# Delta rule on one core: the second head of each pair inverted through the off-diagonal quadrants, P and T in two banks each without a second buffer

## The chip, the core and the metric

One core of a Trainium2 chip (trn2) runs the whole program in one launch. The metric is the device time of one execution in microseconds (us). The engines are PE (TensorE, with PEld for its weight loads), DVE (VectorE), ACT (ScalarE), POOL (GpSimd) and SP (SyncE, which issues DMAs). All arithmetic here is float32; the records of a float32 matmul come in two passes, each a load and a matmul.

## What is computed

The program is a stack of blocks; the part that matters is the RWKV-7 branch of each of the two layers of the second block: six heads of width 64, 1024 tokens, with a state that follows a delta rule.

```python
def step(state, inp):
    r_t, w_t, k_t, v_t, kk_t, a_t = inp
    sa = jnp.einsum('bhvk,bhk->bhv', state, -kk_t)
    state = (state * w_t[:, :, None, :]
             + sa[..., None] * (kk_t * a_t)[:, :, None, :]
             + v_t[..., None] * k_t[:, :, None, :])
    return state, jnp.einsum('bhvk,bhk->bhv', state, r_t)
```

The kernel works through it in chunks of 64 tokens. Within a chunk the recurrence is a triangular system of 64 equations per head, and its unit triangular matrix is inverted by doubling: the inverse T of diagonal blocks of 2 is known at once, and each of five levels (blocks of 4, 8, 16, 32, 64) makes from it a product P with the matrix, masked to the level's blocks, and from P the next T.

## The kernel before

The function `rwkv` (from L2259) is one block of instructions for all engines, written out by hand, with semaphores between them. A tile n is 128 tokens: two chunks of 64, one in SBUF partitions 0 to 63 and one in 64 to 127 (the two slices of `both`). There are NT = 8 tiles a layer, and the function runs once for each of two layers. The six heads are taken in NG = 3 pairs g; with LV = 5 levels that makes K = 15 steps, step k being level k // 3 of pair k % 3. PSUM is the one tensor `bk` of eight banks of 512 columns; the steps use banks 0 to 3, the preceding tile's outputs and state use banks 4 to 7.

A 64 x 64 matmul reads its operands from one half of the partitions and writes to a half. Before the change every matmul of the inversion reads and writes the same half (a diagonal quadrant of the 128 x 128 array). `chunks` (L2711 on) and `carry` also have matmuls that read one half and write the other (off-diagonal quadrants), into another bank than the diagonal ones.

PE's order for a tile n in the main loop at the end of the function: transposes of the inputs (`turns`, L2630), `low`, the preceding tile's `values`, scores of the pairs (`score`, L2642) with `solved` of the preceding tile between, `sums` of the next tile, then `turn_first` for each pair (L2651: the first T is the transpose of TT, its other form), and then the steps. `make_P` (L2661) forms P of both heads of the pair; `make_T` (L2672, L2674) forms the new T and TT; in the last level only TT (L2674). P alternates between banks 0 and 1 (`k % 2`), T between banks 2 and 3.

```python
make_P(n, 0)
for k in range(K):
    if k + 1 < K:
        make_P(n, k + 1)
    next(rest, None)
    make_T(n, k)
```

`rest` is the generator `tail(n - 1)`, the preceding tile's work in pieces: `outputs` (24 matmuls) before T(0), `chunks` of two heads (20 matmuls) before T(1), T(2) and T(3), `carry` (12 matmuls) before T(7) and T(10). The first tile of a layer has none of it.

DVE masks the scores (L2424), makes the first TT of each pair (`first_pairs`, L2429 and L2430), and then in each step masks P into PS (`take_P`, L2435). After take_P(k) it does one piece, and after every third step two, of `side(n)`, the next tile's element-wise work: `exponents` (L2398 to L2404), `keys` (L2381 to L2393, with `take_tr` L2441 among it) and from k = 8 on the four products of `scaled` (L2411 to L2417), which wait for `f_ready`. ACT copies the first T of each pair to SBUF (`take_first`, L2552) and in each step the new T and TT (`take_T`, L2558; L2560 in the last level). From k = 3 on it does pieces of its own `side(n)` after the copy: the next tile's exponentials (`exps`, L2509 and L2513, the last of which sets f_ready, after take_T(7)), `take_r2` (L2533), `take_S` (L2540), `take_y` (L2547). POOL forms five products per tile (`ends`, L2339 to L2343) once f_ready is there. The last tile of a layer has no next tile, so no side work.

What each step waits for, before: P(k) for the copy of that pair's T one level down (take_T(k - 3)); take_P(k) for P(k); T(k) for take_P(k) and, as its bank is reused, for take_T(k - 2); take_T(k) for T(k).

## Time and profile before

| | us |
|---|---|
| runs of the kernel before, median of 3 | 3772.6 (3770.73 to 3773.09) |
| the profiled execution | 3776.29 |
| its span, first to last instruction | 3775.0 |

The profile is that one execution. Times in rows are us from the span's start; a row of the timeline merges instructions of one line that follow each other, and gives its start, its length, the engine, the line, what it writes and reads, how many records, and in brackets how long its engine had been idle before and what ended that. Records of two operations that overlap are split into more rows, and a few matmul records can be missing. The first layer's stage of the delta rule runs from about 2058 to 2285, the second's from 3212 to 3435.

### The profile page before, as it was taken

The page shows a single profiled execution, that of the slowest core. Times are in us where ns is not written, and L with a number is a line of the kernel's source. Part 1 is how long each engine was busy: PE and PEld are TensorE (multiplying, and loading weights), DVE is VectorE, ACT ScalarE, POOL GpSimd, SP SyncE. Part 2 cuts the span into 40 slices and gives each one's busy share as a digit, 9 for nine tenths or more (in the row PEclk, how much of TensorE's full clock was granted, in tenths as well). Part 3 has the DMA queues.
Part 4 walks back from the last instruction along what each step waited for, and adds up shares of the span by engine and source line. Part 5 has one row for each costly group of instructions (what it writes and reads, how often), then busy time and mean ns, then how long its engine had stood idle before and what let it go on. Part 6 is the DMA issues. An engine that isn't in the chain of part 4 may idle for free. (4 is left out here: it accounts for less than half of the span.)

```text
span 3775.0 us, 57764 instructions
## 1 busy us (share of the span) xinstructions
PE 3532.6 (94%) x22960; PEld 2223.4 (59%) x22960; DVE 2164.6 (57%) x4615; ACT 1112.0 (29%) x2461; POOL 512.9 (14%) x326
## 2 busy tenths in 40 slices
PE   7999978999999997999998888998999998888998
PEld 5464444884488544655655776444655655777444
DVE  3255556446764573489976663342389976664343
ACT  2222344220122011320115555222230115555222
POOL 0020232000110010002221211210002221221210
PEclk9999989999999998999998999999999999999999
DMA  7343423234433442113341204211112331313310
GB/s 251 125 132 93 144 101 129 76 104 178 178 104 101 153 179 99 42 49 94 111 146 56 74 23 160 67 63 60 34 51 84 101 120 68 109 32 110 119 63 23
DMA packets 238731, 378.21 MB, mean 100 GB/s; under 512 B 30838, under 2 KB 168062, under 8 KB 237462
## 3 DMA queue, kind: packets, MB, share of 16 engines
q1 hardware_dynamic: 238478, 374.63, 30.2%
q8 instruction: 184, 3.01, 0.3%
q14 instruction: 69, 0.57, 0.1%
HBM read 291.89 MB, written 69.08 MB: 96 GB/s over the span
## 5 line engine op out<-in xcount | busy, mean ns | idle before, releaser
L3816 PE MATMUL win_acc<-across_room,across_hT 128*128 128x384 f32 (+3 forms) x3072 | 908.5, 456 | 3.8 <-PEq L83 3.8
L3816 PEld LDWEIGHTS win_acc<-across_room,across_hT 128*128 128x128 f32 x3072 | 561.4, 191 | 345.5 <-issue 15.5
L2828 DVE TENSOR_SCALAR_CACHE_REDUCE win_over<-d_sc,win_mid 128x384 uint8<-128x384 f32 (+5 forms) x384 | 337.9, 942 | 29.0 <-DVE win_mid L2839 28.6
L3877 ACT ACTIVATE layer_spare<-win_acc 128x384 f32<-128x384 f32 (+1 forms) x144 | 67.3, 467 | 575.4 <-PE win_acc L3816 575.4
L3652 PE MATMUL tail_wo<-tail_w_out,across_room 128*128 128x512 f32 x512 | 229.5, 603 | 6.6 <-DVE across_room L3484 6.6
L3663 PE MATMUL tail_wg<-tail_w_gate,across_room 128*128 128x512 f32 x512 | 224.5, 592 | 2.0 <-DVE across_room L3484 2.0
L3652 PEld LDWEIGHTS tail_wo<-tail_w_out,across_room 128*128 128x128 f32 x512 | 97.7, 193 | 126.0 <-issue 126.0
L1930 PE MATMUL mlp_bk<-across_hT,across_room 128*128 128x256 f32 x768 | 171.0, 379 | 0.0
L3663 PEld LDWEIGHTS tail_wg<-tail_w_gate,across_room 128*128 128x128 f32 x512 | 96.0, 190 | 117.2 <-issue 117.2
L1930 PEld LDWEIGHTS mlp_bk<-across_hT,across_room 128*128 128x128 f32 x768 | 145.9, 190 | 19.8
L3748 POOL TENSOR_TENSOR win_zp<-win_zp,layer_spare 128x3072 f32<-128x3072 f32 (+1 forms) x8 | 44.8, 5594 | 818.0 <-DMA win_zp<-s_z 818.0
L2674 PE MATMUL rwkv_bk<-rwkv_Tb,rwkv_PS 64*64 64x64 f32 x1920 | 127.5, 220 | 10.5 <-DVE rwkv_PS L2435 7.7
L2672 PE MATMUL rwkv_bk<-rwkv_PS,rwkv_Tb 64*64 64x64 f32 x1536 | 110.5, 224 | 24.4 <-DVE rwkv_PS L2435 20.7
L1930 PE MATMUL mlp_bk<-first_big,mlp_sums 128*128 128x256 f32 x512 | 118.8, 386 | 7.8 <-DVE across_room L1612 7.4
L1419 PE MATMUL mid_wo<-across_room,mid_yT 128*128 128x512 f32 x256 | 114.0, 600 | 3.5 <-ACT mid_yT L1360 3.5
L2435 DVE TENSOR_TENSOR rwkv_PS<-rwkv_bk,layer_early 128x128 f32<-128x128 f32 x240 | 67.8, 287 | 86.3 <-PE rwkv_bk L2661 84.7
L3960 DVE SCALAR_TENSOR_TENSOR d_sc<-win_rl,d_iw,d_sc 128x512 f32<-128x512 f32 (+3 forms) x140 | 92.1, 658 | 42.2 <-ACT win_rl L3893 29.1
L2558 ACT ACTIVATE rwkv_Tb<-rwkv_bk 128x256 f32<-128x256 f32 x192 | 73.6, 383 | 143.0 <-PE rwkv_bk L2674 141.9
L497 PE MATMUL zin_acc<-zin_wt,across_hT 128*128 128x272 f32 (+2 forms) x384 | 115.2, 457 | 0.0
L1930 PEld LDWEIGHTS mlp_bk<-first_big,mlp_sums 128*128 128x128 f32 x512 | 98.8, 194 | 22.5 <-issue 8.8
L1571 POOL TENSOR_TENSOR first_big<-first_big,mlp_rows 128x1024 f32<-128x1024 f32 x4 | 9.9, 2464 | 734.1 <-ACT first_big L1838 734.1
L2674 PEld LDWEIGHTS rwkv_bk<-rwkv_Tb,rwkv_PS 64*64 64x64 f32 x1920 | 100.9, 135 | 13.8 <-DVE rwkv_PS L2435 11.8
(578 smaller groups left out, 6630.4 us busy)
## 6 DMA issues: line engine op xcount, KB each, us to landing
across_room<-in_w SPq DMA_DIRECT2D x96, 1024.0 KB, 6.9
across_room<-in_w_in SPq DMA_DIRECT2D x18, 1536.0 KB, 8.2
s_z<-layer_spare SPq DMA_DIRECT2D x14, 1536.0 KB, 6.7
across_room<-in_w_ada SPq DMA_DIRECT2D x8, 2048.0 KB
across_hT<-s_z SPq DMA_DIRECT2D x16, 832.0 KB, 5.4
win_zp<-layer_spare SPq DMA_DIRECT2D x8, 1344.0 KB
tail_w_out<-in_w_out SPq DMA_DIRECT2D x4, 2048.0 KB, 10.8
tail_w_gate<-in_ple_w_gate SPq DMA_DIRECT2D x4, 2048.0 KB, 19.8
```

Source lines behind the costliest of these rows:

```text
L497: mm = pe.matmul(z, w, x, start=k == 0, stop=k == KC - 1)
L1419: mm = pe.matmul(wo[:, n % 2, c, :], yT[:, n % 2, q, :], w_out[:, c, q, :], start=q == 0, stop=q == KC - 1)
L1930: mm = pe.matmul(out, a[:, k, :], b[:, k, :], start=k == 0, stop=k == KC // 2 - 1)
L2435: dve.tensor_tensor(PS[:, 2 * g:2 * g + 2, :], blocks(bk[:, k % 2, 0:2 * HD]), bc_mid(levels[:, q, :], 2), ALU.mult).then_inc(p_out, 1)
L2558: act.activation(Tb[:, n % 2, g, :, :, :].rearrange("p a h t -> p (a h t)"), bk[:, 2 + k % 2, 0:4 * HD], ACT.Copy).then_inc(t_out, 1)
L2672: pe.matmul(bk[pr, 2 + k % 2, col(h)], TT_of(n, 2 * g + h, pr), PS[pr, 2 * g + h, :], start=True, stop=True)
L2674: mm = pe.matmul(bk[pr, 2 + k % 2, col(2 + h)], PS[pr, 2 * g + h, :], TT_of(n, 2 * g + h, pr), start=True, stop=True)
L2828: s.put(dve.tensor_scalar(over[q][:, :], sc[q][:, :], mid[:, q:q + 1], 0.0, ALU.is_gt, ALU.add, accum_out=cnt[:, q:q + 1]))
L3652: mm = pe.matmul(wo[:, c, :], yT[:, n % 2, q, :], W["out"][:, q, c * COL:(c + 1) * COL], start=q == 0, stop=q == KC - 1)
L3663: mm = pe.matmul(wg[:, c, :], xT[:, n % 2, q, :], W["gate"][:, q, c * COL:(c + 1) * COL], start=q == 0, stop=q == KC - 1)
L3816: mm = pe.matmul(acc[:, u % RING, 0:w], hT[:, k, t * P:(t + 1) * P], wt[:, i % 2, k, 0:w], start=k == 0, stop=k == KC - 1)
L3960: dve.scalar_tensor_tensor(x, y, iw, x, ALU.mult, ALU.add).then_inc(summed, 1)
```

## The change

Quoted are the edits that carry it; the two lambdas that swap which half of `Tb` holds T and which TT, and the index changes that follow from that, are left out where nothing else changes.

```diff
+        flat = bk[:, :, :].rearrange("p b c -> p (b c)")
+        T_AT, P_AT = 1 * 512, 3 * 512
+        swapped = [(slice(0, 64), slice(64, 128)), (slice(64, 128), slice(0, 64))]
...
-                    dve.tensor_tensor(mT[:, n % 2, h, :, :], blocks(bk[:, (3, 0, 1, 2, 3, 0)[h], 0:4 * HD]), masks[:, :, :], ALU.mult).then_inc(masked, 1)
+                    dve.tensor_tensor(mT[:, n % 2, h, :, :], blocks(bk[:, (0, 1, 2, 3, 0, 1)[h], 0:4 * HD]), masks[:, :, :], ALU.mult).then_inc(masked, 1)
...
-                    dve.tensor_tensor(PS[:, 2 * g:2 * g + 2, :], blocks(bk[:, k % 2, 0:2 * HD]), bc_mid(levels[:, q, :], 2),
+                    dve.tensor_tensor(PS[:, 2 * g:2 * g + 2, :], blocks(flat[:, P_AT - HD:P_AT + HD]), bc_mid(levels[:, q, :], 2),
...
-                    act.activation(xT[:, q, :, :], pairs(bk[:, q, :]), ACT.Copy).then_inc(xT_ready, 1)
+                    act.activation(xT[:, q, :, :], pairs(bk[:, 1 + q, :]), ACT.Copy).then_inc(xT_ready, 1)
...
-                def take_first(n, g):
-                    act.wait_ge(T_turned, START + NG * n + g + 1)
-                    act.activation(Tb[:, n % 2, g, 0, :, :], blocks(bk[:, 1 + g, 0:2 * HD]), ACT.Copy).then_inc(t_out, 1)
+                def take_first(n):
+                    act.wait_ge(T_turned, START + 2 * n + 1)
+                    act.activation(Tb[:, n % 2, 0, :, :, :].rearrange("p a h t -> p (a h t)")[:, HD:4 * HD], flat[:, P_AT - HD:P_AT + 2 * HD], ACT.Copy).then_inc(t_out, 1)
+
+                def take_others(n):
+                    act.wait_ge(T_turned, START + 2 * n + 2)
+                    act.activation(Tb[:, n % 2, 1:3, 0, 1, :], blocks(bk[:, 1, 0:2 * HD]), ACT.Copy)
+                    act.activation(Tb[:, n % 2, 1:3, 1, :, :].rearrange("p g h t -> p g (h t)"), pairs(bk[:, 0, 0:4 * HD]), ACT.Copy).then_inc(t_out, 2)
...
-                        act.activation(Tb[:, n % 2, g, :, :, :].rearrange("p a h t -> p (a h t)"), bk[:, 2 + k % 2, 0:4 * HD], ACT.Copy).then_inc(t_out, 1)
+                        act.activation(Tb[:, n % 2, g, :, :, :].rearrange("p a h t -> p (a h t)"), flat[:, T_AT - 3 * HD:T_AT + HD], ACT.Copy).then_inc(t_out, 1)
...
-                    banks = ((3, 0), (1, 2), (3, 0))[g]
+                    banks = ((0, 1), (2, 3), (0, 1))[g]
...
-                def turn_first(n, g):
-                    pe.wait_ge(TT_first, START + NG * n + g + 1)
-                    pe.wait_ge(masked, START + RWH * n + 3 + g)
+                def turn_first(n):
+                    pe.wait_ge(TT_first, START + NG * n + 1)
+                    pe.wait_ge(masked, START + RWH * n + 4)
+                    for pr, po in swapped:
+                        pe.matmul(flat[po, P_AT - HD:P_AT], id64[pr, :], TT_of(n, 1, pr), start=True, stop=True)
                     for h in range(2):
                         for pr in both:
-                            mm = pe.matmul(bk[pr, 1 + g, col(h)], Tb[pr, n % 2, g, 1, h, :], id64[pr, :], start=True, stop=True)
+                            mm = pe.matmul(flat[pr, P_AT + h * HD:P_AT + (h + 1) * HD], TT_of(n, h, pr), id64[pr, :], start=True, stop=True)
+                    mm.then_inc(T_turned, 1)
+
+                def turn_others(n):
+                    pe.wait_ge(TT_first, START + NG * n + NG)
+                    pe.wait_ge(masked, START + RWH * (n + 1))
+                    for g in (1, 2):
+                        for pr, po in swapped:
+                            pe.matmul(bk[po, 1, col(g - 1)], id64[pr, :], TT_of(n, 2 * g + 1, pr), start=True, stop=True)
+                        for h in range(2):
+                            for pr in both:
+                                mm = pe.matmul(bk[pr, 0, col(2 * g - 2 + h)], TT_of(n, 2 * g + h, pr), id64[pr, :], start=True, stop=True)
                     mm.then_inc(T_turned, 1)
 
                 def make_P(n, k):
                     g = k % NG
                     pe.wait_ge(t_out, START + (K + NG) * n + k + 1)
-                    if k == 0:
-                        pe.wait_ge(masked, START + RWH * (n + 1))
-                    for h in range(2):
-                        for pr in both:
-                            mm = pe.matmul(bk[pr, k % 2, col(h)], mT[pr, n % 2, 2 * g + h, 0, :], T_of(n, 2 * g + h, pr), start=True, stop=True)
+                    if k >= 1:
+                        pe.wait_ge(p_out, START + n * K + k)
+                    for pr, po in swapped:
+                        pe.matmul(flat[pr, P_AT - HD:P_AT], mT[pr, n % 2, 2 * g, 0, :], T_of(n, 2 * g, pr), start=True, stop=True)
+                        mm = pe.matmul(flat[po, P_AT:P_AT + HD], mT[pr, n % 2, 2 * g + 1, 0, :], T_of(n, 2 * g + 1, pr), start=True, stop=True)
                     mm.then_inc(p_made, 1)
 
                 def make_T(n, k):
                     g = k % NG
+                    a, b = 2 * g, 2 * g + 1
                     pe.wait_ge(p_out, START + n * K + k + 1)
-                    if k >= 2:
-                        pe.wait_ge(t_out, START + (K + NG) * n + NG + k - 1)
-                    for h in range(2):
-                        if k < K - NG:
+                    pe.wait_ge(t_out, START + (K + NG) * n + NG + k)
+                    if k < K - NG:
+                        for pr, po in swapped:
+                            pe.matmul(flat[pr, T_AT - HD:T_AT], TT_of(n, a, pr), PS[pr, a, :], start=True, stop=True)
+                            pe.matmul(flat[po, T_AT:T_AT + HD], TT_of(n, b, pr), PS[pr, b, :], start=True, stop=True)
+                        for h, at in ((a, 3), (b, 2)):
                             for pr in both:
-                                pe.matmul(bk[pr, 2 + k % 2, col(h)], TT_of(n, 2 * g + h, pr), PS[pr, 2 * g + h, :], start=True, stop=True)
-                        for pr in both:
-                            mm = pe.matmul(bk[pr, 2 + k % 2, col(2 + h)], PS[pr, 2 * g + h, :], TT_of(n, 2 * g + h, pr), start=True, stop=True)
+                                mm = pe.matmul(flat[pr, T_AT - at * HD:T_AT - at * HD + HD], PS[pr, h, :], TT_of(n, h, pr), start=True, stop=True)
+                    else:
+                        for pr, po in swapped:
+                            pe.matmul(flat[pr, T_AT - HD:T_AT], PS[pr, a, :], TT_of(n, a, pr), start=True, stop=True)
+                            mm = pe.matmul(flat[po, T_AT:T_AT + HD], PS[pr, b, :], TT_of(n, b, pr), start=True, stop=True)
                     mm.then_inc(t_made, 1)
...
-                        for g in range(NG):
-                            turn_first(n, g)
+                        turn_first(n)
+                        turn_others(n)
                         make_P(n, 0)
                         for k in range(K):
                             if k + 1 < K:
                                 make_P(n, k + 1)
+                            make_T(n, k)
                             next(rest, None)
-                            make_T(n, k)
                     for _ in rest:
                         pass
 
```

`flat` is `bk` with its banks as one row of columns, so that a product's two heads can lie at the end of one bank and the start of the next and be read as one operand: P at the border of banks 2 and 3, T and TT at that of banks 0 and 1. The first head's product goes to the lower bank from diagonal quadrants, the second head's to the upper bank from off-diagonal ones. Each of P and T has one place for all steps now, so make_P(k) waits for take_P(k - 1) and make_T(k) for take_T(k - 1). The second head's chunks lie with their halves swapped in one of its two forms, which is why turn_first and turn_others have two matmuls more for each pair. In PE's order, the piece of `rest` now comes after make_T(k).

## Rows read from the trace of the kernel before

**Rows 1.** Both stages by windows: busy us and records (PE, PEld, DVE, ACT, POOL), clock, DMA, GB/s.
```profile
2058.00:2285.00 227.00, 198.26 (x5441) 175.34 (x5443) 135.73 (x342) 117.41 (x275) 53.88 (x48) 0.99 0.21 61
3212.00:3435.00 223.00, 198.80 (x5467) 175.61 (x5468) 135.79 (x342) 117.12 (x275) 54.41 (x49) 0.99 0.22 62
```

**Rows 2.** Timeline of ACT, tile n = 2 of the second layer (first take_P at 3274.46).
```profile
3276.56 0.38 ACT L2558 ACTIVATE rwkv_Tb<-rwkv_bk 128x256 f32<-128x256 f32 x1 [2.31 <-PE rwkv_bk L2674]
...
3280.76 0.38 ACT L2558 ACTIVATE rwkv_Tb<-rwkv_bk 128x256 f32<-128x256 f32 x1 [1.02 <-PE rwkv_bk L2674]
...
3285.12 0.83 ACT L2513 ACTIVATE layer_spare<-layer_spare 128x768 f32<-128x768 f32 x1
...
3292.24 0.28 ACT L2560 ACTIVATE rwkv_Tb<-rwkv_bk 128x128 f32<-128x128 f32 x1 [0.24 <-PE rwkv_bk L2674]
```

**Rows 3.** Timeline of DVE, the same tile.
```profile
3274.46 0.29 DVE L2435 TENSOR_TENSOR rwkv_PS<-rwkv_bk,layer_early 128x128 f32<-128x128 f32 x1 [1.19 <-PE rwkv_bk L2661]
...
3285.99 0.56 DVE L2411 TENSOR_TENSOR layer_spare<-across_hT,layer_spare 128x384 f32<-128x384 f32 x1 [1.34 <-ACT layer_spare L2513]
3286.46 0.28 DVE L2435 TENSOR_TENSOR rwkv_PS<-rwkv_bk,layer_early 128x128 f32<-128x128 f32 x1
3286.66 1.17 DVE L2413 TENSOR_TENSOR layer_spare<-across_hT,layer_spare 128x384 f32<-128x384 f32 x1
...
3289.05 0.28 DVE L2435 TENSOR_TENSOR rwkv_PS<-rwkv_bk,layer_early 128x128 f32<-128x128 f32 x1
...
3290.34 0.47 DVE L2435 TENSOR_TENSOR rwkv_PS<-rwkv_bk,layer_early 128x128 f32<-128x128 f32 x2
```

**Rows 4.** Timeline of PE, the same tile, steps 1 and 2.
```profile
3275.88 0.28 PE L2672 MATMUL rwkv_bk<-rwkv_PS,rwkv_Tb 64*64 64x64 f32 x4
...
3276.34 0.34 PE L2661 MATMUL rwkv_bk<-rwkv_Tb,rwkv_mT 64*64 64x64 f32 x5
3276.47 0.27 PE L2717 MATMUL rwkv_bk<-rwkv_uw,rwkv_be 64*64 64x64 f32 x1
...
3276.82 0.27 PE L2717 MATMUL rwkv_bk<-rwkv_uw,rwkv_be 64*64 64x64 f32 x1
...
3277.28 0.28 PE L2672 MATMUL rwkv_bk<-rwkv_PS,rwkv_Tb 64*64 64x64 f32 x4
```

**Rows 5.** Timeline of PE, the same tile, the first P and a late step.
```profile
3273.96 0.68 PE L2661 MATMUL rwkv_bk<-rwkv_Tb,rwkv_mT 64*64 64x64 f32 x16 [0.19 <-ACT rwkv_Tb L2552]
...
3289.38 0.33 PE L2672 MATMUL rwkv_bk<-rwkv_PS,rwkv_Tb 64*64 64x64 f32 x4 [0.16 <-DVE rwkv_PS L2435]
```

**Rows 6.** Timeline of DVE, first tile of the second layer.
```profile
3223.12 0.29 DVE L2435 TENSOR_TENSOR rwkv_PS<-rwkv_bk,layer_early 128x128 f32<-128x128 f32 x1 [1.01 <-PE rwkv_bk L2661]
...
3223.91 0.29 DVE L2435 TENSOR_TENSOR rwkv_PS<-rwkv_bk,layer_early 128x128 f32<-128x128 f32 x1
```

**Rows 7.** Timeline of ACT, first tile of the second layer, the last exponential.
```profile
3230.44 0.84 ACT L2513 ACTIVATE layer_spare<-layer_spare 128x768 f32<-128x768 f32 x1
```

**Rows 8.** Timeline of DVE, last tile of the first layer.
```profile
2270.29 0.29 DVE L2435 TENSOR_TENSOR rwkv_PS<-rwkv_bk,layer_early 128x128 f32<-128x128 f32 x1
2270.99 0.29 DVE L2435 TENSOR_TENSOR rwkv_PS<-rwkv_bk,layer_early 128x128 f32<-128x128 f32 x1 [0.41 <-PE rwkv_bk L2661]
```

**Rows 9.** Windows: busy us and records by engine, clock, DMA share, GB/s.
```profile
2160.10:2163.50 3.40, 1.80 (x59) 1.66 (x55) 1.35 (x4) 1.21 (x3) 0.00 (x0) 1.00 0.19 69
2163.50:2166.90 3.40, 2.99 (x59) 2.81 (x57) 2.22 (x5) 2.23 (x5) 2.09 (x2) 0.50 0.02 5
3285.00:3290.40 5.40, 3.95 (x121) 3.64 (x115) 4.42 (x8) 2.77 (x8) 4.28 (x4) 1.00 0.01 3
```

**Rows 10.** Timeline of PE around the fall of the clock, first layer.
```profile
2163.22 0.21 PE L2674 MATMUL rwkv_bk<-rwkv_Tb,rwkv_PS 64*64 64x64 f32 x1 [1.60 <-issue]
...
2163.71 0.52 PE L2674 MATMUL rwkv_bk<-rwkv_Tb,rwkv_PS 64*64 64x64 f32 x4
2163.93 0.52 PE L2672 MATMUL rwkv_bk<-rwkv_PS,rwkv_Tb 64*64 64x64 f32 x4
```

More of the change, by code:

```diff
@@ L2299, in rwkv @@
         both = (slice(0, 64), slice(64, 128))
-        T_of = lambda n, h, pr: Tb[pr, n % 2, h // 2, 0, h % 2, :]
-        TT_of = lambda n, h, pr: Tb[pr, n % 2, h // 2, 1, h % 2, :]
+        T_of = lambda n, h, pr: Tb[pr, n % 2, h // 2, 1, h % 2, :]
+        TT_of = lambda n, h, pr: Tb[pr, n % 2, h // 2, 0, h % 2, :]
+        flat = bk[:, :, :].rearrange("p b c -> p (b c)")
+        T_AT, P_AT = 1 * 512, 3 * 512
+        swapped = [(slice(0, 64), slice(64, 128)), (slice(64, 128), slice(0, 64))]
         with ph.block() as block:
@@ L2429, in first_pairs @@
                     s(dve.scalar_tensor_tensor(L, L, -1.0, bc_mid(id64[:, :], 2), ALU.mult, ALU.add))
-                    dve.tensor_tensor(Tb[:, n % 2, g, 1, :, :], L, bc_mid(first[:, :], 2), ALU.mult).then_inc(TT_first, 1)
+                    dve.tensor_tensor(Tb[:, n % 2, g, 0, :, :], L, bc_mid(first[:, :], 2), ALU.mult).then_inc(TT_first, 1)
                 def take_P(n, k):
@@ L2557, in take_T @@
                     if k < K - NG:
-                        act.activation(Tb[:, n % 2, g, :, :, :].rearrange("p a h t -> p (a h t)"), bk[:, 2 + k % 2, 0:4 * HD], ACT.Copy).then_inc(t_out, 1)
+                        act.activation(Tb[:, n % 2, g, :, :, :].rearrange("p a h t -> p (a h t)"), flat[:, T_AT - 3 * HD:T_AT + HD], ACT.Copy).then_inc(t_out, 1)
                     else:
-                        act.activation(Tb[:, n % 2, g, 1, :, :], blocks(bk[:, 2 + k % 2, 2 * HD:4 * HD]), ACT.Copy).then_inc(t_out, 1)
+                        act.activation(Tb[:, n % 2, g, 0, :, :], blocks(flat[:, T_AT - HD:T_AT + HD]), ACT.Copy).then_inc(t_out, 1)
                 def side(n):
@@ L2591, in _ @@
                         if n < NT:
-                            for g in range(NG):
-                                take_first(n, g)
+                            take_first(n)
+                            take_others(n)
                             for k in range(K):
@@ L2629, in turns @@
                         for m in range(4):
-                            mm = pe.transpose(bk[:, q, m * P:(m + 1) * P], x4[:, m, q * P:(q + 1) * P], ident[:, :])
+                            mm = pe.transpose(bk[:, 1 + q, m * P:(m + 1) * P], x4[:, m, q * P:(q + 1) * P], ident[:, :])
                         mm.then_inc(turned, 1)
                 def score(n, g):
-                    banks = ((3, 0), (1, 2), (3, 0))[g]
+                    banks = ((0, 1), (2, 3), (0, 1))[g]
                     if g < 2:
@@ L2776, in _ @@
                     if n < NT:
-                        for g in range(NG):
-                            turn_first(n, g)
+                        turn_first(n)
+                        turn_others(n)
                         make_P(n, 0)
```

## The prediction

> **What bounds the kernel now.** I read the page's busy line first, then the windows of the two stages that the change touches, then one tile of the second layer, engine by engine. The delta rule fills 450 us of the 3775 us span (two layers, eight tiles of 128 tokens each); PE is busy 397 of them, at a clock of 0.99 [rows 1]. So a share of PE's time looks worth saving, but one tile shows that PE bounds only part of the stage. A tile takes 450/16 = 28 us: a head of transposes, scores and masks, and then, for 18 us, 15 steps k (five levels for each of three pairs of heads). A step is a product P, its masking by DVE (take_P), a product T and its copy by ACT (take_T).
>
> The steps have three limits. *Early (k = 0 to 4)* PE sets the pace, because the preceding tile's outputs and chunks are done between the steps: the first copy of T starts at 3276.56 and the fourth 4.20 us later [rows 2], 1.40 a step, which is P, T and two heads of chunks. *Middle (k = 5 to 8)* ACT does its copy and an exponential in each step, and at k = 8 DVE stands idle 1.34 us until the last exponential is out [rows 3]. *Late (k = 9 to 11)* DVE alone sets the pace, 1.30 us a step: take_P plus a 1.17 us product [rows 3]. The last three steps are a chain of hand-offs between engines.
>
> **Part 1: the second head goes to the off-diagonal quadrants.** Now two matmuls (one on each diagonal quadrant, four records, since float32 takes two passes) take 0.117 us: T's four pairs start at 3275.88 and P follows 0.46 us later [rows 4]. P is two pairs, T four (two in the last level). The only place of this kernel that uses all four quadrants is the chunks: ten matmuls of one head, six diagonal and four off-diagonal, start 0.35 us apart from head to head [rows 4], just the time of the three diagonal pairs. So off-diagonal work costs nothing beside diagonal work, if it goes to another bank, which is what the change provides. After: P 0.12, T 0.35 (one four-quadrant round and two diagonal pairs), 0.12 in the last level. Each step gives PE back 0.23 to 0.24 us, 15 x 16 x 0.235 = 56 us in all. That is the gross gain; the rest of this part asks how much reaches the end. A burst of P alone after a wait is not in the trace, so I bound P: 0.12 (the chunks' overlap) to 0.23 (no overlap). I take 0.12, as the chunks issue the same pattern of matmuls.
>
> **Part 2: one buffer each for P and T.** P(k+1) now waits for take_P(k), and T(k) for take_T(k-1). This makes two loops. Hand-offs are 0.05 us (DVE ends 3289.33 [rows 3], PE starts 3289.38 [rows 5]), a waiting PE starts 0.05 later than a streaming one (0.33 against 0.28 for a group), and the last matmul ends 0.16 after its pair's slot [rows 4, 5].
> P loop: 0.05 + 0.05 + 0.12 + 0.16 + 0.05 + 0.29 = 0.72 us. T loop: 0.05 + 0.05 + 0.35 + 0.16 + 0.05 + 0.38 = 1.04 us, 0.71 in the last level. The P loop is under DVE's usual 0.79 [rows 6], so it costs nothing until DVE's side work ends. The T loop is over it and becomes the limit wherever PE and DVE were quicker. The tail work and P(k+2) are queued behind T(k) and wait with it; behind P(k+2) stands DVE's side work.
>
> **Part 3: T moves ahead of the tail work in PE's queue.** T(k) no longer stands behind outputs (1.40 us, before k = 0), chunks (0.70) or carry (0.70). The copies get earlier by that, once; outputs and carry have slack.
>
> **A middle tile, step by step** (12 of 16, times from its first take_P at 3274.46). Before: f_ready, the last exponential, at 11.49; take_P(9) 12.00; take_P(12) 15.88; last copy 18.06 [rows 2, 3]. After: PE issues P(1), T(0) until 0.87, outputs until 2.27, then three steps of 0.47 + 0.70; T(3) is issued at 5.08 and copied at 5.29, against 6.30 before. Then ACT and the T loop: copies at 6.46, 7.50, 8.54 and 9.58, with exponentials between, so f_ready is at 10.69, 0.80 earlier; of the 1.0 us that PE gained, the T loop has eaten 0.2. DVE's late steps are the same, so take_P(12) comes at 15.10. Then the second P is missing: take_P(13) came 0.20 after take_P(12) (two in 0.47 us [rows 3]), and now follows a whole P loop later, and take_P(14) again; with the copies the last one ends at 17.64. Gain 0.42 us.
>
> **The head.** Bank numbers rotate with no new wait. The first pair's T, which P(0) waits for [rows 5], has its copy now 192 columns wide instead of 128, about 0.05 us more: copies take 0.28 for 128 and 0.38 for 256 columns [rows 2]. The other pairs wait for the third first_pairs, as the third turn did; their 12 matmuls (six new off-diagonal ones per tile) and two copies end before T(0) needs them, under ACT's idle 2.31 us [rows 2]. Without that cover they would cost up to 0.4 us a tile. Net per middle tile: -0.42 + 0.05 = **-0.37**, x12 = -4.4 us.
>
> **First tile of a layer** (no tail work, two of them). PE never bound it: DVE did, at 0.79 a step [rows 6]. The T loop replaces that: copies 1.04 apart, so f_ready moves from 8.16 [rows 7] to about 9.46, +1.30; with the tail's loss of 0.36 that is +1.7 each, +3.4. **Last tile** (nothing ahead, two): PE's 0.70 a step [rows 8] becomes 1.04 in six steps, +2.0, against 0.94 from the first four; +1.1 each, +2.2. DMA queues, POOL and SP are passed by no step.
> Sum of the parts: -4.4 + 3.4 + 2.2 = **+1.2 us**. The 56 us of PE time buy almost nothing.
>
> **The clock.** PE that is given back work stands idle instead. In steps 9 to 12 of the middle tile PE is busy 3.95 of 5.40 us at full clock [rows 9]. The change takes four times 0.235 us away and joins each P to its T (one end of 0.16 less, four times): 2.4 of 5.4. Before the one place inside the loops where the granted clock fell, PE had been busy 1.80 of 3.40 us; the next 3.4 us ran at 0.50, 1.2 GHz [rows 9], and pairs took 0.21 [rows 10]. I expect such falls here. One costs between nothing (inside DVE-bound steps) and 1.7 us (3.4 us of a PE-bound head at half speed); I take 1.0, since the T loop at 0.21 a pair is 1.4 us against DVE's 1.30 and the stretch may reach into the next head. I take eight falls in 16 tiles, between one as now and one in each: **+8 us**.
> The Trainium skill, "TensorE: Matmul & The Clock Gate", section "A second HAM failure mode: psum-queue depth-cycling", says that PE pausing briefly as it cycles through PSUM makes the gate go to and fro; by it there would be a fall in nearly every tile, some +14 us, while the trace of before has one.
> Total +9 us. The profiled execution took 3776.3 us (span 3775.0 and 1.3 around it), 3.7 over the median of 3772.6; the change is put on the median: **3782 us**.
>
> **Rivals.**
> *Balance.* The clock holds; the sum is +1.2 (from -5 to +7 by the bounds on the head): 3774. For it: the one fall came after a pause of 1.60 us [rows 10], longer than any that a step has. Chance 0.25.
> *Faster.* The T copies don't bind. If T plus copy is back under DVE's 0.79 (the wait overlapping the matmuls' start), the whole 0.80 at f_ready reaches the end, and the outer tiles lose nothing: 12 x -0.8 = -9.6, 3763. Against it: 0.35 + 0.38 alone are 0.73. Chance 0.14.
> *Quadrants start one after another.* If a burst's starts follow in line, its price is one start each: 17.5 ns as the chunks' 20 records in 0.35 us, to 29 ns as the two-quadrant bursts' four in 0.117. At 17.5 ns P is 0.14 and nothing changes; at 29 ns P is 0.23 and T 0.47, there is no gain at all (the change doesn't do what it says) and only single buffers remain: about +1.7 in a middle tile and +3.4 in the others, +34, 3807. Chance 0.05 for that, 0.12 for something between, near 3788 (P 0.18: f_ready 0.5 later, 0.1 more in each last step).
> The Trainium skill, same page, section "Wait — 56ns, not 53.3ns?", gives a floor of about 25 ns from start to start; an estimate by that page is P 0.20 and T 0.40, about +16 us. The chunks' 17.5 ns [rows 4] go below it.
>
> **How the numbers follow.** Forecast 0.44 (3777 to 3790 with one to 14 falls), balance 0.25, faster 0.14, starts in line 0.17. The measurement of this kernel tells about 0.2% from no change, 7.5 us. Faster by more: most of that rival and a bit of balance, 0.13. Within: most of balance, the low end of the forecast, 0.33. Slower: the rest, 0.54. The range goes from 3765 to 3798; it leaves out the lack of any overlap and the ends of the rivals.
>
> **What would show it.** Right: P bursts of eight records within 0.12 us; copies of T never under 1.04 us apart up to k = 11; DVE's wait at k = 8 ending some 0.8 us earlier from the first take_P; 0.72 between the last take_Ps; a granted clock under 1.00 in windows of the loops. Wrong: a last copy at 17 us or less from the first take_P, PE bursts at 29 ns a start, or a clock of 1.00 all through both stages.

## The result, and the profile of the changed kernel

The changed kernel takes 3840.5 us (median of 4 runs, 3829.9 to 3851.2) against 3772.9 for the kernel before: a ratio of 1.018, with a 95% interval of 1.0164 to 1.0195. It is slower, as forecast, but by 68 us where 9 were predicted, and outside the range. The profiled execution took 3846.1 us (span 3844.8). One of the four executions of a later experiment, e9_single_T, took 9335.6 us for a reason that is not known; its figures below are of the other three.

The loss is in the two stages of the delta rule. From their first PE record to their last they took 231.0 and 226.6 us before and take 267.3 and 267.2 now. Both stages by windows, columns as in [rows 1]:

```profile
2056.10:2323.40 267.30, 222.79 (x5631) 188.28 (x5631) 136.68 (x342) 124.30 (x277) 56.22 (x52) 0.83 0.18 52
3240.80:3508.00 267.20, 224.63 (x5631) 189.34 (x5631) 136.69 (x342) 124.02 (x278) 55.97 (x52) 0.81 0.18 52
```

DVE is busy as long as in [rows 1], within 1 us. PE was to lose 56 us of busy time over both stages and has gained 45 (402.5 to 447.4 from the first record to the last), mostly because its clock is 0.83 and 0.81 where it was 0.99. Since the clock's record in these traces has only 1.00 and 0.50, 0.83 over 267 us means some 91 us at 1.2 GHz; over both stages the clock's record has 195 us at 0.50, against 12 before. One tile of the second layer (n = 1) shows where, in windows of its head (transposes, scores and masks), the first 10 us of its loop, the rest of the loop, and the next tile's head:

```profile
3270.73:3281.23 10.50, 10.33 (x160) 7.96 (x160) 4.87 (x15) 6.36 (x13) 0.00 (x0) 0.84 0.01 2
3281.23:3291.20 9.97, 8.04 (x344) 7.53 (x344) 6.92 (x18) 4.01 (x10) 0.00 (x0) 1.00 0.26 79
3291.20:3303.60 12.40, 10.64 (x212) 9.13 (x206) 6.06 (x12) 5.86 (x15) 6.18 (x5) 0.50 0.12 42
3303.60:3314.67 11.07, 10.89 (x160) 8.11 (x160) 4.87 (x14) 6.37 (x13) 0.00 (x0) 0.79 0.55 146
```

The clock falls in the loop, stays at 0.50 for its last 12.4 us, and comes back only inside the next head, which takes 11.07 us; at full clock a head takes 8.90, as before (8.93). Nearly every tile looks like this: the clock is low somewhere in 14 of the 16 loops and in 15 heads, where before it was so in one loop and two heads. The prediction had eight falls of 3.4 us.

The tile of [rows 2 to 5] has its first take_P at 3314.67 now. Its copies of T on ACT (timeline, k = 0, 3, 4, 5, 6, 7):

```profile
3315.86 0.38 ACT L2566 ACTIVATE rwkv_Tb<-rwkv_bk 128x256 f32<-128x256 f32 x1 [0.99 <-PE rwkv_bk L2696]
...
3320.60 0.38 ACT L2566 ACTIVATE rwkv_Tb<-rwkv_bk 128x256 f32<-128x256 f32 x1 [1.32 <-PE rwkv_bk L2696]
...
3321.82 0.38 ACT L2566 ACTIVATE rwkv_Tb<-rwkv_bk 128x256 f32<-128x256 f32 x1 [0.43 <-PE rwkv_bk L2696]
...
3322.96 0.38 ACT L2566 ACTIVATE rwkv_Tb<-rwkv_bk 128x256 f32<-128x256 f32 x1
...
3324.10 0.38 ACT L2566 ACTIVATE rwkv_Tb<-rwkv_bk 128x256 f32<-128x256 f32 x1 [0.37 <-PE rwkv_bk L2696]
...
3325.24 0.38 ACT L2566 ACTIVATE rwkv_Tb<-rwkv_bk 128x256 f32<-128x256 f32 x1
```

The first comes 1.19 us after take_P(0), against 2.10 in [rows 2]: T(0) is no longer behind the outputs. The fourth comes at 5.93 (6.30 before, 5.29 predicted), and from the fifth on they are 1.14 apart, where the T loop was to be 1.04. So the last exponential, which sets f_ready, is not earlier: it ends 12.8 us after the first take_P (median of the 12 middle tiles), against 12.1 before; the prediction had it 0.80 earlier, at 10.69. PE's burst of the first P of that tile (timeline):

```profile
3314.26 0.27 PE L2681 MATMUL rwkv_bk<-rwkv_Tb,rwkv_mT 64*64 64x64 f32 x1
3314.27 0.27 PE L2682 MATMUL rwkv_bk<-rwkv_Tb,rwkv_mT 64*64 64x64 f32 x1
...
3314.39 0.22 PE L2682 MATMUL rwkv_bk<-rwkv_Tb,rwkv_mT 64*64 64x64 f32 x1
```

DVE's last take_Ps (timeline) in a tile whose loop ran at full clock, n = 4 of the first layer:

```profile
2212.91 0.28 DVE L2438 TENSOR_TENSOR rwkv_PS<-rwkv_bk,layer_early 128x128 f32<-128x128 f32 x1
2213.74 0.29 DVE L2438 TENSOR_TENSOR rwkv_PS<-rwkv_bk,layer_early 128x128 f32<-128x128 f32 x1 [0.55 <-PE rwkv_bk L2682]
2214.58 0.29 DVE L2438 TENSOR_TENSOR rwkv_PS<-rwkv_bk,layer_early 128x128 f32<-128x128 f32 x1 [0.55 <-PE rwkv_bk L2682]
```

Eight records start within 0.13 us, so the quadrants overlap as predicted. The P loop is 0.83 to 0.84 us instead of 0.72; in [rows 3] two take_Ps there took 0.47 together.

### The profile page after: what moved, and what is told of

Its sections match the earlier page's. It is cut to its first block and busy times, and to the rows that moved or that the text cites. A ratio compares the mean times of both kernels' runs of the same rounds, so it can differ in the third digit from the quotient of the medians.

```text
span 3844.8 us, 58372 instructions
## 1 busy us (share of the span) xinstructions
PE 3569.0 (93%) x23152; PEld 2244.9 (58%) x23152; DVE 2156.8 (56%) x4615; ACT 1123.4 (29%) x2461; POOL 512.5 (13%) x326
## 5 line engine op out<-in xcount | busy, mean ns | idle before, releaser
L2681 PE MATMUL rwkv_bk<-rwkv_Tb,rwkv_mT 64*64 64x64 f32 x960 | 96.5, 258 | 30.4 <-DVE rwkv_PS L2438 20.9
L2696 PE MATMUL rwkv_bk<-rwkv_Tb,rwkv_PS 64*64 64x64 f32 x1536 | 102.0, 246 | 0.6 <-issue 0.5
L2682 PE MATMUL rwkv_bk<-rwkv_Tb,rwkv_mT 64*64 64x64 f32 x960 | 97.2, 269 | 2.0 <-issue 2.0
```

Of the source, the lines that this page charges most:

```text
L2681: pe.matmul(flat[pr, P_AT - HD:P_AT], mT[pr, n % 2, 2 * g, 0, :], T_of(n, 2 * g, pr), start=True, stop=True)
L2682: mm = pe.matmul(flat[po, P_AT:P_AT + HD], mT[pr, n % 2, 2 * g + 1, 0, :], T_of(n, 2 * g + 1, pr), start=True, stop=True)
L2696: mm = pe.matmul(flat[pr, T_AT - at * HD:T_AT - at * HD + HD], PS[pr, h, :], TT_of(n, h, pr), start=True, stop=True)
```

## The experiments

Three theories: **clock** (PE's pauses cost it its clock, and that is the loss), **waits** (the single buffers' loops are the loss) and, from the first results on, **supply** (PE runs out of instructions). All results together; the stage length is from the first to the last PE record that writes the delta rule's banks, both layers; low is the part of it at a clock of 0.50; stalls are PE's idle times there that no engine ended ("issue" in the view of waits). The loop of a middle tile runs from its first take_P to its last copy of T, mean of 12.

| kernel | median us | ratio, 95% | stages us | low us | stalls us | middle loop us |
|---|---|---|---|---|---|---|
| before | 3772.9 | 1 | 457 | 12 | 10 | 18.9 |
| changed | 3840.5 | 1.018 (1.0164 to 1.0195) | 534 | 195 | 17 | 22.0 |
| e1_twice | 3888.0 | 1.0307 (1.0288 to 1.0325) | 581 | 78 | 55 | 25.6 |
| e2_single | 3825.4 | 1.0137 (1.0117 to 1.0156) | 512 | 37 | 10 | 21.7 |
| e3_order | 3866.9 | 1.025 (1.0232 to 1.0269) | 556 | 244 | 16 | 23.3 |
| e4_fill | 3812.8 | 1.0108 (1.009 to 1.0126) | 502 | 56 | 22 | 21.5 |
| e5_long | 3815.6 | 1.0114 (1.0096 to 1.0132) | 491 | 16 | 19 | 20.7 |
| e7_before_order | 3764.0 | 0.9983 (0.9973 to 0.9994) | 455 | 18 | 9 | 18.7 |
| e8_single_P | 3813.9 | 1.0113 (1.0094 to 1.0131) | 494 | 29 | 10 | 21.4 |
| e9_single_T | 3816.7 | 1.0118 (1.0095 to 1.0141) | 499 | 18 | 8 | 20.8 |
| e10_swap | 3843.6 | 1.0179 (1.0162 to 1.0196) | 537 | 206 | 16 | 21.7 |
| e11_swap_fill | 3806.7 | 1.0094 (1.0077 to 1.0111) | 491 | 31 | 16 | 20.5 |
| e12_merged | 3790.1 | 1.0048 (1.0032 to 1.0065) | 474 | 19 | 7 | 19.4 |
| e13_mixed_order | 3764.7 | 0.9971 (0.9961 to 0.9982) | 447 | 12 | 9 | 18.1 |

Each ratio is against the kernel before on the same chip (medians 3770.5 to 3775.1).

### Single buffers without the quadrants

**e2_single**: the kernel before, with one place each for P and T and T ahead of the tail work, both heads on the diagonal as before (P always in bank 0, T in bank 2). Its edit, without the bank numbers:

```diff
                         pe.wait_ge(masked, START + RWH * (n + 1))
+                    else:
+                        pe.wait_ge(p_out, START + n * K + k)
...
-                    if k >= 2:
-                        pe.wait_ge(t_out, START + (K + NG) * n + NG + k - 1)
+                    pe.wait_ge(t_out, START + (K + NG) * n + NG + k)
...
-                            next(rest, None)
                             make_T(n, k)
+                            next(rest, None)
```


> The kernel before with the waits of the change alone: P in one bank, T in one bank, T ahead of the tail's piece, second head on the diagonal quadrants as before. Clock theory: PE has as much work as before, so the clock stays near 0.97; the loops cost what the prediction gave for no overlap, about 34 us: 3800 to 3815 us. Quadrant theory: four quadrants at once lower the clock by themselves; then this one is at 0.97 too, but so is not the doubled-burst kernel. Wait theory: the single buffers alone cost nearly all, 3830 to 3850 us.

The time lies between the ranges of the clock theory and the wait theory: +1.37%, 52 us, with 37 us at low clock. So the buffers and the order carry most of the loss without any quadrant, and the quadrants, which take PE work away, add 16 us more.

**e8_single_P** and **e9_single_T** take the first or the second of these three pieces alone, with its bank.

> The kernel before with one buffer for P (P(k+1) waits for take_P(k)) and nothing else changed. Wait theory with the prediction's hand-offs: a P loop of 0.05 + 0.05 + 0.23 + 0.16 + 0.05 + 0.29 = 0.83 us costs 0.6 a tile at take_P(13) and little elsewhere: 3780 to 3787 us. If hand-offs are larger than predicted (loop 0.92, as the run with both single buffers shows): 3787 to 3800 us.

> The kernel before with one buffer for T (T(k) waits for take_T(k-1)) and nothing else changed. Wait theory: a T loop of 0.05 + 0.05 + 0.47 + 0.16 + 0.05 + 0.38 = 1.16 us against 0.79 in the three middle steps and in the outer tiles: +1.1 in a middle tile, +3.4 in the four outer ones, 3785 to 3800 us. If the two single buffers cost nothing one by one and only their sum with the order does: within 8 us of 3772.

e8 gives 3814, above both of its ranges; e9 gives 3817, above its own. Each buffer alone costs 43 and 45 us (by the ratios) at nearly full clock, and both with the turned order 52: they do not add up. Both delay the same last exponential: it ends 12.1 us after the first take_P before, 13.3 in e8, 13.0 in e9 and 13.7 in e2 (medians of 12 middle tiles). Both also lengthen the same last two steps: from copy to copy of T these take 1.1 us together before, 1.5 in e8, and 1.8 in e9 and in e2. How much each of the two explains was not worked out. In e8 a middle tile's steps against those of before (median us from take_P to take_P): k = 0 0.99 (0.79), k = 1 2.03 (1.54), k = 6 and 7 0.98 (0.79), k = 8 2.70 (2.56), k = 11 1.57 (1.29), k = 12 0.92 (0.20), together 2.2. In e9 three copies of T on ACT (timeline of a middle tile, second layer, n = 6, k = 4 to 6):

```profile
3417.82 0.38 ACT L2558 ACTIVATE rwkv_Tb<-rwkv_bk 128x256 f32<-128x256 f32 x1 [0.77 <-PE rwkv_bk L2673]
...
3419.07 0.38 ACT L2558 ACTIVATE rwkv_Tb<-rwkv_bk 128x256 f32<-128x256 f32 x1
...
3420.31 0.38 ACT L2558 ACTIVATE rwkv_Tb<-rwkv_bk 128x256 f32<-128x256 f32 x1 [0.48 <-PE rwkv_bk L2673]
```

1.25 apart, where the prediction's hand-offs gave 1.16 and DVE had set 0.79.

### The order alone

**e3_order**: the changed kernel with the tail work ahead of T again. **e7_before_order**: the kernel before with T ahead of it. **e13_mixed_order**: the same from step 1 on, whose edit is shown (e7 has make_T first for every k, e3 exchanges the two lines in the changed kernel).

```diff
-                            next(rest, None)
+                            if k == 0:
+                                next(rest, None)
                             make_T(n, k)
+                            if k > 0:
+                                next(rest, None)
```


> The changed kernel with the tail's piece ahead of make_T again, as before the change. All theories: T(k) and its copy come up to 0.7 us later where a piece stands in front (k = 1 to 3, 7), so the last exponential is 0.7 us later in a tile: 10 to 15 us slower than the changed kernel, 3848 to 3858 us. If it is not slower, the order is not what carries the middle of a tile.

> The kernel before with T(k) ahead of the tail work in PE's queue and nothing else changed (double buffers, diagonal quadrants). Prediction's part 3 (the order only moves the first copies once): 3768 to 3775 us. Order theory (the reversed order in the changed kernel cost 26 us, so the order is worth as much by itself): 3745 to 3760 us. Clock as before, 0.97.

> The kernel before with T(k) ahead of the tail work in PE's queue from step 1 on, and in step 0 behind it as it was. In the run with T ahead in every step T(0) waited for take_P(0) with the outputs behind it, and take_P(2) came 0.38 us later (1.92 against 1.54 from take_P(1)), while DVE's wait at step 8 shrank from 2.56 to 2.12. If both can be had, take_P(2) is back at 1.54 and step 8 stays near 2.12 to 2.2: 0.3 to 0.38 in 12 middle tiles, 4 us less than 3764, 3758 to 3762 us, faster than both kernels. Rival (ACT's copies and exponentials set the end of step 8, so what step 1 gains is lost at step 8): 3763 to 3767 us.

e3 is worse than expected, with 244 us at low clock. e7 is 3764.0, below the first range and above the second: the order by itself gains 0.17%. In its middle tiles step 8 shrinks from 2.56 to 2.12, as part 3 of the prediction meant, but step 1 grows from 1.54 to 1.92: T(0) waits for take_P(0), and the outputs and P(2) stand behind it. e13 keeps both, 1.54 and 2.12: DVE's wait for the last exponential, 1.34 in [rows 3], is 0.90 in most tiles of e13 and 0.99 in this one (timeline):

```profile
3272.80 0.56 DVE L2411 TENSOR_TENSOR layer_spare<-across_hT,layer_spare 128x384 f32<-128x384 f32 x1 [0.99 <-ACT layer_spare L2513]
```

It takes 3764.7 us where the kernel before took 3775.1 beside it, a ratio of 0.9971. The time itself is just above the expected 3762, the kernel before being slower on that chip too; the ratio is the better measure. The time alone would fit the rival's range as well, but step 8 has lost nothing. e13 is 0.3% faster than the kernel before, clear of noise; that it is faster than e7 is shown by the step and not by the times, whose intervals overlap.

### The clock

**e1_twice** issues each four-quadrant burst twice. **e4_fill** puts 2 to 4 dummy pairs of 64 columns into a free bank behind the tail work (k = 6 to 13, first tile from 0), **e5_long** one pair of 160 or 320 columns. The first piece below is e1's (before each burst's loop, which it indents), the other two are e5's.

```diff
+                    for _ in range(2):
                     for pr, po in swapped:
...
                             next(rest, None)
+                            fill(n, k)
...
+                    w = 320 if 9 <= k <= 11 else 160
+                    for pr in both:
+                        pe.matmul(bk[pr, 5, 0:w], mT[pr, n % 2, 0, 0, :], mT[pr, n % 2, 0:2, :, :].rearrange("p h m t -> p (h m t)")[:, 0:w], start=True, stop=True)
```


> The changed kernel with each four-quadrant burst issued twice (all of P, and T's first round), the second time over the same values: 240 x 0.12 us or more of extra PE work for P and as much for T, some 56 us in all, all of it on the two loops. Clock theory: most of the 68 us is the clock, which falls because PE stands idle; doubled bursts keep PE as busy as before the change, the granted clock comes back from 0.95 to 0.97 or more, and the kernel gets FASTER than the changed one, about 3805 to 3820 us. Wait theory: the 68 us are the single buffers' waits and the clock is a side effect; every doubled burst lengthens a loop by 0.12 us, and the kernel is slower than the changed one, 3855 to 3885 us.

> The changed kernel with filler matmuls behind the tail's piece from k = 6 on (from k = 0 in the first tile of a layer): two diagonal pairs a step, four for k = 9 to 11, into a bank that nobody reads then; their results are not used. They are PE work of 0.23 to 0.47 us a step where PE waits. Clock theory: the clock stays up (0.97), and the time falls to 3785 to 3800 us, although PE does more. Wait theory: nothing gained, 3840 to 3850 us.

> The changed kernel with one pair of longer dummy matmuls (160 columns, 320 in steps 9 to 11) behind the tail work of each step from k = 6 to 13 (first tile: 0 to 13), 16 instructions a tile where the run with short fillers had 44, for about the same PE time. Clock theory (the excess is mostly the low clock): the clock holds as with the short fillers or better (stage low for under 56 us), and with fewer instructions the stalls of PE without a visible cause fall from 22 to about 12 us: 3790 to 3803 us. Wait theory (the single buffers' waits are what costs): as with the short fillers, 3810 to 3825 us, whatever the clock.

e1 brought much of the clock back (78 us low) and is slower than either theory said: its stalls went from 17 to 55 us. e4 took 28 us off the time with more work for PE, so the low clock is a cause, though the time is above the 3800 that the clock theory allowed; it still had 56 us low. e5 holds the clock, as both stages by windows show:

```profile
2054.80:2298.50 243.70, 211.95 (x5911) 175.81 (x5911) 136.72 (x342) 122.61 (x277) 56.18 (x52) 0.99 0.20 57
3218.80:3466.50 247.70, 212.88 (x5911) 176.71 (x5911) 136.84 (x342) 122.64 (x277) 56.37 (x52) 0.98 0.19 56
```

Its heads are back at 8.9 us. The quadrant theory named with e2 (four quadrants at once lower the clock by themselves) is out with that: e5 has all of them and 16 us at low clock. But the time is 3815.6, no better than e4, 13 above what the clock theory expected and within the wait theory's range: with the clock held, most of the loss is still there. Part of the rest is the dummies' own: its step 12 takes 1.00 us instead of 0.83.

### The hand-off

**e10_swap** exchanges the two waits of make_P. **e11_swap_fill** has that and dummies only in steps 6 to 11 (320 columns from step 8 on).

```diff
-                    pe.wait_ge(t_out, START + (K + NG) * n + k + 1)
                     if k >= 1:
                         pe.wait_ge(p_out, START + n * K + k)
+                    pe.wait_ge(t_out, START + (K + NG) * n + k + 1)
```


> The changed kernel with the two waits of make_P in the other order (take_P's first, T's copy second) and nothing else. Hand-off theory: of two waits on one matmul the second in the program is an instruction of its own, 0.12 us from take_P's end to the first weight load instead of 0.05; with the order turned the one that comes last rides on the matmul. Then the last take_Ps come 0.07 to 0.1 us closer (0.83 to 0.75 us at full clock), some five steps of a tile bound by this loop, 16 tiles: 5 to 8 us less, 3830 to 3836 us; the clock stays as low as it is. Rival (the hand-off is the same whatever the order): periods unchanged, 3835 to 3845 us.

> The changed kernel with the waits of make_P turned and dummy matmuls that hold the clock only where PE stands idle anyway (steps 6 and 7: 160 columns, 8 to 11: 320, none in the last steps). Clock theory with both refinements: heads at 8.9 us, last steps back to 0.75 to 0.83, 3795 to 3805 us. What remains over 3772 would be the single buffers' loops and the stalls on instructions. If the clock falls again without the dummies of steps 12 and 13: 3810 to 3830 us.

The hand-off theory is right about the loop. PE's weight load behind the take_P of 2213.74 above, changed kernel (timeline):

```profile
2214.14 0.13 PEld L2681 LDWEIGHTS rwkv_bk<-rwkv_Tb,rwkv_mT 64*64 64x64 f32 x1 [0.47 <-ACT rwkv_Tb L2568]
```

The same place of the same tile in e10, PE's weight load:

```profile
2219.08 0.13 PEld L2681 LDWEIGHTS rwkv_bk<-rwkv_Tb,rwkv_mT 64*64 64x64 f32 x1 [0.43 <-DVE rwkv_PS L2438]
```

And DVE's last take_Ps there:

```profile
2217.99 0.28 DVE L2438 TENSOR_TENSOR rwkv_PS<-rwkv_bk,layer_early 128x128 f32<-128x128 f32 x1
2218.73 0.29 DVE L2438 TENSOR_TENSOR rwkv_PS<-rwkv_bk,layer_early 128x128 f32<-128x128 f32 x1 [0.47 <-PE rwkv_bk L2682]
2219.49 0.29 DVE L2438 TENSOR_TENSOR rwkv_PS<-rwkv_bk,layer_early 128x128 f32<-128x128 f32 x1 [0.47 <-PE rwkv_bk L2682]
```

In the changed kernel take_P ends at 2214.03 (2213.74 and 0.29) and the first weights load 0.11 later; the trace has a semaphore instruction of 0.05 us between, for make_P's second wait. In e10 they load 0.06 after take_P's end at 2219.02, and take_P is named as the releaser. take_Ps are 0.74 to 0.76 apart instead of 0.83 to 0.84. Yet e10's time is not below the changed kernel's (1.0179 against 1.018) and lies in the rival's range. It spent 206 us at low clock, 11 more than the changed kernel, so that a lower clock may have taken back what the shorter loop gave; this is not shown. With the clock held, e11 is the best version with quadrants whose output is complete, 1.0094, 34 us under the changed kernel and just above the 3805 expected. Without the dummies of steps 12 and 13 it has 31 us at low clock, against 16 in e5.

### The instructions

**e12_merged**: e5 with the preceding tile's outputs and chunks done for two heads in one matmul; the first matmul of outputs is shown, the others are changed alike. The second head of each two goes through the first one's operand, so the kernel leaves out the second head's own products.

```diff
-                    for h in range(RWH):
+                    for h in range(0, RWH, 2):
+                        at = slice(col(h).start, col(h).start + P)
                         for pr in both:
-                            pe.matmul(bk[pr, 7, col(h)], mT[pr, n % 2, h, 1, :], uw[pr, h, 0:HD], start=h == 0, stop=False, skip_group_check=True)
+                            pe.matmul(bk[pr, 7, at], mT[pr, n % 2, h, 1, :], uw[pr, h:h + 2, 0:HD], start=h == 0, stop=False, skip_group_check=True)
```


> The kernel with the longer dummy matmuls, and the preceding tile's outputs and chunks done for two heads in one matmul of 128 columns instead of two of 64: the columns are the same, the matmuls 42 a tile fewer (this part of the result is not that of the reference). Supply theory (the stalls of PE without a visible cause are PE waiting for its own instructions, which come in packets): the stalls fall from 19 us to under 6 in the two stages, and the time by 13 us or more against the run with longer dummies, 3790 to 3800 us. Rival (the stalls have another cause, that goes with PE's time): 16 to 20 us of stalls as there, 3805 to 3816 us.

3790.1 us, 26 less than e5 (the profiled executions differ by 22, their stages by 18), with the stalls at 7.3 us, just over the 6 expected. The line of PE's idle time in the delta rule's banks that nothing visible ended (from the view of that tile on PE: us, times) is, in the changed kernel

```profile
  issue: 17.2, 21
```

in e1

```profile
  issue: 55.3, 60
```

in e5

```profile
  issue: 19.0, 24
```

and in e12

```profile
  issue: 7.3, 9
```

The supply theory holds: 12 us fewer stalls for the same columns. The steps of chunks, clear of stalls, are 1.14 instead of 1.17 too, so not all of the 26 us are stalls. The last exponential of a middle tile ends 11.0 us after the first take_P, against 12.8 in e5.

The stalls can be seen with their cause in a stretch of e5 in which almost nothing but instructions is moved. PE after its stalls (timeline):

```profile
3288.69 0.27 PE L2755 MATMUL rwkv_bk<-across_hT,rwkv_ke 64*64 64x64 f32 x1 [1.22 <-issue]
...
3292.72 0.27 PE L2754 MATMUL rwkv_bk<-layer_ident,rwkv_rf 64*64 64x64 f32 x1 [1.48 <-issue]
```

The view of DMA of the same run, in 40 slices of 0.25 us from 3285.70 on, and its instruction queue:

```profile
GB/s 66 0 0 0 0 0 0 0 0 0 0 0 0 0 0 0 0 66 0 0 0 0 0 0 0 0 0 0 0 0 0 0 0 66 0 266 133 53 106 293
...
q8 instruction: 3, 0.05, 2.7%
```

Three packets of 16 KB start at 3285.77, 3290.11 and 3294.16 and take 1.4 us each. PE resumes at 3288.69 and 3292.72, 1.5 and 1.2 us after one has landed. Between, it runs 126 matmuls in 2.55 us (20 ns each) and then stands 1.48 us without any: 4.03 us, 32 ns a matmul, however fast it could go.

## Why the prediction was wrong

**Right.** The direction; four-quadrant bursts of P in 0.12 us (0.13); the early steps at 1.17 (predicted 0.47 + 0.70, measured 1.17 where PE did not stall); first copies earlier; the head, which takes 8.90 us at full clock (8.93 before); the mechanism of the clock, though the falls start in steps 6 to 10 in 12 of the tiles, where the prediction named the steps from 9 on.

**The clock** was one of two mis-sized terms. It was taken as eight falls of 3.4 us at 1.0 us each, +8. The runs show 195 us at low clock in nearly all tiles, reaching from the second half of the loop into the next head, which alone lengthens the heads of 16 tiles by 23 us (143.2 to 166.5, from a head's first PE record to the first take_P). Holding the clock is worth 0.85% of the time (1.0179 in e10 to 1.0094 in e11, which has the dummies besides), some 32 us. The prediction took the length of a fall from the only one in the loops of before [rows 9]. Why that one was so short is not shown: PE was as busy in it (2.99 of 3.40 us) as in the 12.40 us above (10.64). The cited rule of the Trainium skill ("TensorE: Matmul & The Clock Gate", section "A second HAM failure mode: psum-queue depth-cycling") agrees with the trace: a clock that goes to and fro tile by tile. The prediction's estimate by it, +14, came near the count of falls (18 start in the two stages) and made each too short (they last 3.4 to 17.1 us).

**The loops** were the other, and by the larger error: +1.2 us in the sum of the parts, some +35 in e11, with the clock held and make_P's waits exchanged (the stalls and what its dummies cost are in it), and +52 in e2 with diagonal heads. Four steps of it failed.
- *"The P loop is under DVE's usual 0.79 [rows 6], so it costs nothing until DVE's side work ends."* It is 0.84 in the last steps and 0.91 in steps 0, 6 and 7. The hand-off of 0.05 was read from T in [rows 5], whose wait for take_P rides on the matmul. In make_P that wait is the second of two and an instruction of its own: 0.11 to the weight load and 0.15 to the first matmul. That is 0.10 of the 0.12 by which the loop is longer; e10, which exchanges the two, gets 0.08 of it back (0.74 to 0.76). The other terms of the loop were right to 0.02.
- *The T loop of 1.04* is 1.14 (1.25 with diagonal heads in e9). Its wait for take_T is the second of two as well, which may cost the same; exchanging it was not tried.
- *Part 3, "outputs and carry have slack".* They may have; P(2), queued behind the outputs, has not: step 1 grew to 1.81, and to 1.92 in e7. e13 shows it by leaving step 0 alone.
- *The outer tiles*, +1.7 and +1.1 in the sum: their loops grew from 16.2 to 19.4 us in e11 on average, +3.2.

In a middle tile (-0.42 predicted for the loop) nothing is gained at full clock: the cleanest loop of e11, with one stall in it, takes 19.4 us, against 18.06 to 18.3 of the clean ones before.

**PE's own rate** was no term of the sum at all. The gross gain of 56 us assumed that PE can start matmuls as fast as quadrants allow. In the early steps it cannot keep that up: it runs out of instructions. e12 gives the price: with 42 matmuls fewer in a tile than e5, the last exponential ends at 11.0 instead of 12.8, near the 10.69 of the prediction, and the loop is 1.3 us shorter. The pause of 1.60 us [rows 10], which the prediction used as an argument for the rival in which the clock holds, was such a stall: PE resumed 1.5 us after an instruction packet had landed, at 2161.73.

**The rivals.** *Balance* and *faster* are out. *Starts in line* is out by the 0.13 us bursts, though its price for single buffers alone, +34, was nearer than the forecast's +1.2. The chance for slower, 0.54, should have been larger: a change that takes work from an engine which doesn't set the end, and pays with waits on the chain that does, has little to win.

**Open.** How the 16 us between e2 and the changed kernel divide is argued, not shown: the quadrants take PE work away, and low clock grows from 37 to 195 us. A kernel with quadrants and two buffers each was not tried; with two banks for each buffer, as here, it would need eight, and the loops have four.

## What to carry to other kernels

Take work from an engine only where that engine sets the end; elsewhere it can turn into pauses, and those into a lower clock for work that does count. Before a buffer is given up, work out its loop with the hand-offs of that very instruction: the wait that comes last in time belongs first in the program, and what is queued behind it counts. In stretches of small matmuls read the stalls that nothing visible ends, and try fewer, wider matmuls before faster ones.

## What had not been expected of the hardware

PE waited for its own instructions. In six traces (before, changed, e1, e4, e5, e7) there are 131 idle times over 0.4 us in these stages that no engine ended. Every one ends 1.2 to 1.6 us after a 16 KB packet of the instruction queue has landed; the next packet starts at least 1.05 us after PE has resumed. Two packets never start closer than 3.2 us there, in any of the six. In all 14 traces there are 227 such idle times, within the same bounds. That these are PE's own instructions shows in their count: the queue has 88 packets in the two stages before and 120 in e1, one for every 126 of PE's matmul records in both. The Trainium skill ("Runtime: NRT & Kernel Launch", section "Instruction fetch mechanics") says that instructions come in 16 KiB blocks of 256 while the engine works on, and that the cost of a block's border is mostly hidden. The blocks agree with the trace; that the cost is hidden doesn't where matmuls start 20 ns apart: 10 us of these stages before, 17 in the changed kernel, 55 in e1.

A second wait on one matmul cost 0.08 us in each round of a loop (0.84 to 0.76), and taking it off the path did not show in the time; that the clock took it back is likely, not shown.
